# Two-layer mixer model on one core: reordering the second block's gates, roots, convolutions and parked loads round its quarter products

## The reference

```python
def hybrid_mixer(h, lower_bound, w_in, conv_w, ...):
    proj = h @ w_in                       # 1024 x 8192
    xa, ga, q, f, v, g, m_a, m_b = jnp.split(proj, SPLIT_POINTS, axis=-1)
    xa = causal_depthwise_conv(xa, conv_w, conv_b)        # 4 taps
    y_a = rg_lru(xa, w_r, b_r, w_i, b_i, lam) * jax.nn.gelu(ga)
    ...
    sig = jax.nn.sigmoid(zf)
    log_f = jnp.log(jnp.maximum(lb + (1.0 - lb) * sig, F_MIN))
    kf = (1.0 - lb) * jax.nn.sigmoid(-zf)
    o = rms_norm(hgrn2_chunkwise(qf, kf, log_f, vf), hg_norm)
    y_b = o * jax.nn.silu(g)
    y = jax.nn.sigmoid(m_a) * y_a + jax.nn.sigmoid(m_b) * y_b
    return y @ w_out
# rg_lru: r, i = sigmoid(block products of x); log_a = -8 r softplus(-lam); a = exp(log_a)
#         u = sqrt(max(-expm1(2 log_a), 0)) * (i * x); h = scan(a, u)
```

## Time and profile before

| | us |
|---|---|
| median of 3 runs | 3155.71 (3154.32 to 3157.86) |
| the profiled execution's own time | 3158.05 |
| its span, first to last instruction | 3156.2 |
| PE busy | 2902.3 (92%) |
| DVE busy | 1993.8 (63%) |
| ACT busy | 1290.2 (41%) |
| POOL busy | 1279.4 (41%) |

### The profile page before, as it was taken

The page is one execution under the profiler, slowest core; times in us unless marked ns, Lnnn a source line. Parts: engine busy times, 40 slices in busy tenths (PEclk is TensorE's granted clock), DMA queues, the critical chain, the costliest instruction groups (busy, mean ns, idle before and its releaser), DMA issues.

```text
span 3156.2 us, 49864 instructions
## 1 busy us (share of the span) xinstructions
PE 2902.3 (92%) x20118; PEld 1811.5 (57%) x20118; DVE 1993.8 (63%) x3135; ACT 1290.2 (41%) x2321; POOL 1279.4 (41%) x1071
## 2 busy tenths in 40 slices
PE   7979998999879989998889989989987999999998
PEld 7529875874449658754555655654653444444444
DVE  2476897763589987645875666576564474444445
ACT  2353655653366646633444444443532222222222
POOL 2402472010604570002745646656553335555552
PEclk9999999999999999999999999999998999999999
DMA  7323241002202330021101101101113101111111
GB/s 247 135 66 108 97 144 55 15 18 107 97 1 81 128 104 16 25 87 60 54 27 41 67 27 54 54 27 54 55 41 147 54 17 58 49 51 53 54 54 74
DMA packets 50901, 213.49 MB, mean 68 GB/s; under 512 B 4681, under 2 KB 9969, under 8 KB 34033
## 3 DMA queue, kind: packets, MB, share of 16 engines
q1 hardware_dynamic: 42288, 195.63, 17.5%
q10 hardware_dynamic: 8384, 14.68, 1.4%
HBM read 190.36 MB, written 19.94 MB: 67 GB/s over the span
## 4 chain that ended last, share of the span: by engine, by line
PE 72%; DVE 19%; issue 4%; ACT 4%; DMA 1%; POOL 0%; ACTq 0%; SPq 0%; DVEq 0%; POOLq 0%
PE big L282 15%; PE big L283 14%; PE big L284 14%; PE banks L282 5%; PE banks L284 5%; PE banks L283 5%; PE banks L1175 3%; DVE arena L2002 2%; PE banks L1002 2%; DVE arena L2246 1%; PE big L674 1%; DVE arena L2385 1%; DVE arena L2336 1%; DVE arena L2226 1%; PE banks L677 1%
## 5 line engine op out<-in xcount | busy, mean ns | idle before, releaser
L644 POOL TENSOR_TENSOR w_lo<-stage,w_hi 128x512 bf16<-128x512 f32 x340 | 423.6, 1276 | 368.3 <-ACT w_hi L1373 368.1
L637 POOL CAST w_hi<-stage 128x512 bf16<-128x512 f32 x252 | 178.7, 749 | 793.7 <-PE big L284 600.4
L587 POOL TENSOR_TENSOR w_lo<-stage,w_hi 128x512 bf16<-128x512 f32 x180 | 256.6, 1436 | 351.2 <-ACT w_hi L1573 269.5
L282 PE MATMUL big<-w_hi,ht_hi 128*128 128x256 bf16 (+2 forms) x1280 | 353.3, 285 | 15.2 <-DVE arena L1833 4.7
L282 PE MATMUL big<-ht_hi,w_hi 128*128 128x512 bf16 x800 | 309.1, 386 | 49.4 <-ACT arena L1587 17.9
L283 PE MATMUL big<-w_lo,ht_hi 128*128 128x256 bf16 (+2 forms) x1280 | 353.0, 285 | 0.0
L284 PE MATMUL big<-w_hi,ht_lo 128*128 128x256 bf16 (+2 forms) x1280 | 352.9, 285 | 0.0
L283 PE MATMUL big<-ht_lo,w_hi 128*128 128x512 bf16 x800 | 308.8, 386 | 0.0
L284 PE MATMUL big<-ht_hi,w_lo 128*128 128x512 bf16 x800 | 308.3, 385 | 0.0
L282 PE MATMUL big<-arena,w_hi 128*128 128x512 bf16 (+1 forms) x728 | 232.1, 335 | 45.8 <-DVE arena L2355 21.9
L283 PE MATMUL big<-arena,w_hi 128*128 128x512 bf16 (+1 forms) x728 | 231.4, 334 | 0.0
(11 more groups left out here) (390 smaller groups left out, 7245.4 us busy)
## 6 DMA issues: line engine op xcount, KB each, us to landing
stage<-in_w SPq DMA_DIRECT2D x130, 1024.0 KB, 4.8
arena<-in_w_ada SPq DMA_DIRECT2D x48, 512.0 KB, 3.9
arena<-in_x SPq DMA_DIRECT2D x16, 512.0 KB, 7.4
xs<-arena SPq DMA_DIRECT2D x16, 512.0 KB, 2.6
arena<-xs SPq DMA_DIRECT2D x16, 512.0 KB, 8.5
gt<-arena ACTq DMA_DIRECT2D x16, 256.0 KB, 2.8
arena<-gt ACTq DMA_DIRECT2D x16, 256.0 KB, 2.6
out_x<-arena SPq DMA_DIRECT2D x8, 512.0 KB, 2.6
```

Source lines behind the costliest of these rows:

```text
L282: pe.matmul(out, ah, bh, start=start, stop=False, skip_group_check=onto)
L587: return pool.tensor_tensor(lo, x, hi, ALU.subtract)
L637: pool.tensor_copy(w_flat[0][:, w0 + c0:w0 + c1], stage[:, n % RAW_RING, c0:c1]).then_inc(s_w_hi_split, mark(s_w_hi_split, n, q))
L644: ins = pool.tensor_tensor(w_flat[1][:, w0 + c0:w0 + c1], stage[:, n % RAW_RING, c0:c1], w_flat[0][:, w0 + c0:w0 + c1], ALU.subtract)
```

## The change

Seven edits, all in the second block:

1. The reciprocal on DVE goes. ACT makes the reciprocal root as exp(-0.5 ln(x)): `mean_log` in step ss for c = 0 (in `ga`) and `root_power` in `mb` behind "u1"; for c = 1 both in the next `xa` behind "u1" (`reciprocal_root`). `normed_state` of c = 0 moves from behind c11 to behind c12 of `mb`.
2. The input gate's arithmetic on DVE is taken apart and put between levels 4, 5 and 6. ACT does tanh and exponential of a half right behind its gate. The tanh of the first half is kept in `KT_`.
3. The two roots in `ga` are parted: the first behind "u2", the second behind "p5". The gelu of `ga` moves into `mb` behind "u1".
4. In `xa`, `y2_low(b-1, 0)` moves from behind c11 to behind c22 on DVE, and `y2_high(b-1, 0)` from "u1" to "u2" on ACT.
5. In `f`, the second convolution is cut in two halves, behind c11 and behind c22. ACT's second `forget` moves behind "u1" of `q`.
6. For `b` = 0: ACT copies the first half of `xa` out before it makes further sums; DVE makes the low parts of sum t1 before the first convolution, runs `forget` inside `q` (behind c22 and c12) and the second convolution behind `q`. The high and low parts of the second half of the convolution move into `v`.
7. Of the parked tiles four are loaded at the end of the last `mb`, two in the last `ma` behind "p5", with a semaphore of their own, and the tiles' places are swapped accordingly.

```diff
-        Y2_AT = [27648, 28672, 12288, 29704, 16384, 18432, 6144, 7168]
+        Y2_AT = [27648, 28672, 16384, 18432, 12288, 29704, 6144, 7168]
...
             def first_two(part, g):
-                pe.wait_ge(s_y2_in, when(s_y2_in))
                 for p, ks in ((0, range(4)), (1, range(2))):
+                    if p:
+                        pe.wait_ge(s_y2_rest, when(s_y2_rest))
+                    else:
+                        pe.wait_ge(s_y2_in, when(s_y2_in))
...
+            def functions(c, b, func, start=512):
+                act.wait_ge(s_c_out, when(s_c_out, c, b, "c12"))
+                act.wait_ge(s_p_out, when(s_p_out, c, b, "c21"))
+                for m, x0 in enumerate((0, start)):
+                    y = {"q": QE, "ga": YS, "mb": IT, "gg": FG, "ma": TH}[c][m][:, x0:T]
+                    act.activation(y, y, func).then_inc(...)
+            def tanh_r(b, m):
+                act.activation((KT_, TH[1])[m], R_[m], ACT.Tanh, scale=...)
...
+            def mean_log(b, c):
+                for half in range(2):
+                    act.activation(KT_[half], tile("t", "hs", b, c, "ss", half), ACT.Ln, scale=1.0 / P, bias=s_(S_EPS))
+            def reciprocal_root(b, c):
+                mean_log(b, c)
+                root_power(b, c)
+            def root_power(b, c):
+                act.activation(KT_, KT_, ACT.Exp, scale=-0.5)
@@ scalar, b == 0 @@
-                    sums_to_tt(0, "t2", "t3", "t4")
+                    sums_to_tt(0, "t2")
+                    evac(XAP[:, 0, 3:1027], ACT.Copy, "xa", 0, 0)
+                    sums_to_tt(0, "t3", "t4")
+                    evac(XAP[:, 1, 3:1027], ACT.Copy, "xa", 0, 1)
+                    parts_high(SEVEN[0], (0, 1, 2))
+                    parts_high(SEVEN[0], (3, 5))
+                    sums_to_tt(1, "t2")
+                    parts_high(SEVEN[0], (4,))
+                    parts_high(SEVEN[0], (6,))
                     for c in range(2):
+                        if c:
+                            sums_to_tt(1, "t3", "t4")
+                            act.wait_ge(s_gemm, when(s_gemm, "f", 0, 1))
+                            for g in range(2):
+                                sums_to_tt(g, "t1")
...
@@ scalar, b > 0 @@
-                    seven("xa", b, ACT.Copy, u1=lambda: y2_high(b - 1, 0), c21=lambda: y2_high(b - 1, 1))
+                    seven("xa", b, ACT.Copy, u1=lambda: reciprocal_root(b - 1, 1), u2=lambda: y2_high(b - 1, 0), c21=lambda: y2_high(b - 1, 1))
...
-                    for c in range(2):
-                        forget(b, c)
+                    forget(b, 0)
...
-                seven("q", b, ACT.Silu)
+                seven("q", b, ACT.Silu, u1=(lambda: forget(b, 1)) if b else None)
@@ scalar, gates @@
+                    if n == 0:
+                        tanh_r(b, 0)
                     evac(IT[n], ACT.Sigmoid, "i", b, n, bias=v_("b_i", 2 * b + n))
+                    if n == 1:
+                        tanh_r(b, 1)
+                    act.activation(R_[n], R_[n], ACT.Exp, scale=...)
-                seven("ga", b, ACT.Gelu_apprx_tanh, hgrn, u2=roots)
+                seven("ga", b, ACT.Copy, hgrn, u2=lambda: root(0), p5=lambda: root(1))
+                def between():
+                    root_power(b, 0)
+                    functions("ga", b, ACT.Gelu_apprx_tanh, 0)
-                seven("mb", b, ACT.Sigmoid, hgrn)
+                seven("mb", b, ACT.Sigmoid, hgrn, u1=between, u2=lambda: act.wait_ge(s_rg_dve, when(s_rg_dve, "ha", b, 1)), c21=y2_load if b == 3 else None)
-                seven("ma", b, ACT.Sigmoid, hgrn, c21=y2_load if b == 3 else None)
+                seven("ma", b, ACT.Sigmoid, hgrn, p5=y2_load_rest if b == 3 else None)
+            reciprocal_root(3, 1)
@@ vector @@
             def normed_state(b, m):
-                step(dve.reciprocal(KT_, KT_))
                 dve.scalar_tensor_tensor(OO, OO, v_("hg_norm", 0), KT_, ALU.mult, ALU.mult)
@@ vector, b == 0 @@
-                    conv_2(0, 0)
                     dve.wait_ge(s_gemm, when(s_gemm, "f", 0, 1))
                     for g in range(2):
                         sum_low(g, "t1", TSB[g])
-                    for c in range(2):
-                        forget(0, c)
+                    conv_2(0, 0)
+                    seven("q", 0, c22=(lambda: forget(0, 0),), c12=(lambda: forget(0, 1),))
                     conv_2(0, 1)
-                    seven("q", 0)
@@ vector, b > 0 @@
-                    seven("xa", b, c11=(lambda: y2_low(b - 1, 0), lambda: gated_state(b - 1, 1)), c22=(lambda: recurrent(b - 1, 1),), c12=...)
+                    seven("xa", b, c11=(lambda: gated_state(b - 1, 1),), c22=(lambda: y2_low(b - 1, 0), lambda: recurrent(b - 1, 1)), c12=...)
-                    seven("f", b, c11=(lambda: conv_2(b, 1),))
+                    seven("f", b, c11=(lambda: conv_2(b, 1, range(2)),), c22=(lambda: conv_2(b, 1, range(2, TAPS_2)),))
@@ vector, gates @@
-                seven("v", b, hgrn)
-                for u in range(4):
-                    hgrn(*hsteps[4 + u])
+                seven("v", b, hgrn, c11=(lambda: xs_low(1),))
+                hgrn(*hsteps[4])
+                hgrn(*hsteps[5])
+                input_gate(0)
+                hgrn(*hsteps[6])
+                one_less_square(0)
+                hgrn(*hsteps[7])
+                input_gate(1)
+                one_less_square(1)
-                seven("mb", b, hgrn, c11=(lambda: normed_state(b, 0),))
+                seven("mb", b, hgrn, c12=(lambda: normed_state(b, 0),))
```

More of the change, by code:

```diff
@@ L1692, in hgrn @@
                             freed(s_hgrn_act, "ho", *key, half)
-                    elif st == "ss":
-                        for half in range(2):
-                            act.wait_ge(s_hgrn, when(s_hgrn, *key, half))
-                            act.activation(KT_[:, half * 512:(half + 1) * 512], tile("t", "hs", *key, half)[:, :], ACT.Sqrt, scale=1.0 / P, bias=s_(S_EPS)).then_inc(s_hgrn_act, mark(s_hgrn_act, "o_rms", b, c, half))
-                            freed(s_hgrn_act, "hs", *key, half)
-                seven("v", b, ACT.Copy, hgrn)
+                    elif st == "ss" and c == 0:
+                        mean_log(b, 0)
+                seven("v", b, ACT.Copy, hgrn, u1=lambda: xs_high(1))
+                act.wait_ge(s_rg_dve, when(s_rg_dve, "xc", b, 1))
+                act.wait_ge(s_dve_setup, when(s_dve_setup, "sp8"))
                 for n in range(2):
-                    act.wait_ge(s_rg_dve, when(s_rg_dve, "xc", b, 1))
                     evac(R_[n], ACT.Sigmoid, "r", b, n, bias=v_("b_r", 2 * b + n))
+                    if n == 0:
+                        if b:
+                            act.wait_ge(s_hgrn_dve, when(s_hgrn_dve, "y2_a", b - 1, 1))
+                        else:
+                            act.wait_ge(s_t_lo, when(s_t_lo, "b2", 0, "t1"))
+                        tanh_r(b, 0)
                     if b:
@@ L2419, in _, with xs_low @@
                     normed_state(b - 1, 1)
-                    seven("xa", b, c11=(lambda: y2_low(b - 1, 0), lambda: gated_state(b - 1, 1)), c22=(lambda: recurrent(b - 1, 1),), c12=(lambda: y2_low(b - 1, 1),))
+                    seven("xa", b, c11=(lambda: gated_state(b - 1, 1),), c22=(lambda: y2_low(b - 1, 0), lambda: recurrent(b - 1, 1)), c12=(lambda: y2_low(b - 1, 1),))
                     conv_2(b, 0)
-                    seven("f", b, c11=(lambda: conv_2(b, 1),))
+                    seven("f", b, c11=(lambda: conv_2(b, 1, range(2)),), c22=(lambda: conv_2(b, 1, range(2, TAPS_2)),))
                     seven("q", b, c11=(lambda: forget(b, 0), lambda: forget(b, 1)))
-                for c in range(2):
+                def xs_low(c):
                     dve.wait_ge(s_rg_act, when(s_rg_act, "xs_hi", b, c))
                     dve.tensor_tensor(XS[1][:, c, :], XC[c], XS[0][:, c, :], ALU.subtract).then_inc(s_rg_dve, mark(s_rg_dve, "xs_lo", b, c))
+                xs_low(0)
                 def blocks(x, h):
```

88 lines of the change are left out of this document (45 added, 43 removed).

## The result

The changed kernel takes 3098.69 us (median of 4 runs, 3097.95 to 3101.14); the kernel before took 3155.71 in the same session (median of three runs; a fourth, at 4996.81, is left out as a slow one). The ratio is 0.982 with a 95% interval of 0.9801 to 0.9839, so 1.8% faster. The forecast was 3090, with 3068 to 3112 around it. The profiled execution took 3101.14 us, its span is 3099.3.

What follows compares the result with a forecast made beforehand. PE, busy 92% of the span, was taken as the bound: its work plus its gaps. Terms 25.6 + 30.4 + 3.9 - 5.5 + 12 = 66.4 us off 3158.05 gave 3091.7, by the median 3089.4, predicted 3090 (own range 3080 to 3102; with rivals 3068 to 3112).

Steps and rivals of the forecast that it cites:

- `ga`: 25.6 forecast: PE's four waits for the "p5" copy in `ga` go whole: 17.9 us plus 7.7 of lower clock.
- `mb`: 30.4 forecast: In `mb`, PE's waits for DVE's level 0 go with the reciprocal: 17.4 us plus 13.0 of lower clock.
- gaps in `mb` or `ga` that are only shorter: Sign named in advance as showing the prediction wrong: gaps in `mb` or `ga` shortened instead of gone.
- The slack of 1.3 us: In `mb`, DVE's level 0 would be ready at 1645.1, PE arriving at 1646.4.
- `xa`, `f`, `q`: 3.9 forecast: Last three parts: DVE's chain waits for ACT, POOL's weights bound next; gain 3.9 us, ends 0 and 19.
- the one wait of 3 to 4 us for POOL ahead of `q`: Parts two to four: the gaps of 3.9 + 2.4 us come back as this wait, with the same clock loss.
- The start: -5.5 forecast: First part: a new wait of about 6 us at level 0 for DVE's `qf`; loss 5.5 us, ends -8 and +2.
- The tail: 12 forecast: Behind the last `ma`: parked tiles end no wait, first token tile comes earlier; gain 12 us, ends 9 and 16.
- is split at 2407.2: Tail: POOL, started with the end of `ma`, finishes `o3` then, leaving PE 1.8 us idle.
- its third rival: POOL falls behind, slowed beside DVE by 8.7 us per chunk in `xa`, `f`, `q`: 3168 us, chance 0.04.
- the one for the tail: Sign: the tiles end no wait; `o3` and `y2_low(3, 1)` do, with under 6 us together.
- The rival in which ACT is the bound: ACT's added logarithms, exponentials and table loads delay copies PE waits for, 3 us x 7: 3111 us, chance 0.2.

Runs made afterwards that it cites:

- Experiments 3 to 5: Kernel after with edit 3 undone (3099.14 us), with DVE's half of edit 2 undone (3114.04 us), and with both undone (3113.0 us).
- Experiment 6: Kernel after with the state root of c = 0 by Sqrt and DVE's reciprocal again in all four parts: 3129.33 us.
- Experiments 7 and 12: Kernel after with looser waits ahead of `f` (3089.86 us); with those, a convolution of b=0 earlier, ACT making `o3`'s high parts, convolutions halved over `f` (3078.69 us).
- experiment 9: Kernel after with the state root of the last step (3,1) alone by Sqrt and DVE's reciprocal again: 3096.71 us.
- experiment 10: Kernel after with all six parked tiles loaded at the end of `ma` again, the two semaphores of edit 7 kept: 3099.57 us.
- experiment 5: Kernel after with edit 3 and DVE's half of edit 2 both undone: 3113.0 us.

## Why the prediction was right, and where it was not

The median of 3098.69 lies 9 us above the forecast of 3090 and inside the forecast's own 3080 to 3102.

**`ga`: 25.6 forecast, 25.9 measured.** Counted between step tr and step ss of c = 0, the four gains are 6.1, 6.0, 7.5 and 6.2 us. The mechanism was put down to edits 2 and 3 together. Experiments 3 to 5 part them: edit 3 adds nothing once edit 2 is there, DVE's half of edit 2 carries 10.0 us even with edit 3 in place, and 12.3 us stay when both are undone. The order on ACT in the first `ga` of the kernel after:

```profile
1616.43 1.06 ACT L1756 ACTIVATE arena<-arena 128x1024 f32<-128x1024 f32 x1
1617.39 0.58 ACT L1591 ACTIVATE arena<-big 128x512 f32<-128x512 f32 x1
1618.39 1.05 ACT L1756 ACTIVATE arena<-arena 128x1024 f32<-128x1024 f32 x1
```

The whole part starts 7 us later than before. Less these 7 us, DVE was done with its products at 1605.6 (1612.6), where 1604 to 1608 was forecast, and the copy of p5, which stands between the roots, came at 1610.4 (1617.4), where 1610 to 1611 was forecast.

**`mb`: 30.4 forecast, 27.9 measured.** Of the gap of 4.3 us 0.5 is left in each of the four parts, 2.0 us together, since DVE ended level 0 at 1647.7 and not before PE. By the letter of the prediction ("gaps in `mb` or `ga` that are only shorter") this is a miss, though the lower clock behind it is gone. The slack of 1.3 us that the prediction counted was 1.8 too large: level 0 took 5.0 us on DVE (1642.8 to 1647.7) and not 4.1, two of its operations running at 1.6 us, and began 0.9 us later than counted. Experiment 6 shows the same sum from the other side, 27.7.

**`xa`, `f`, `q`: 3.9 forecast, 5.8 measured.** Counted from step tr of c = 1 to step tr of the next part, the three gave 2.3, 0.9 and 2.6. In the first `xa` DVE's multiply stood 31.8 us behind that step and stands 31.3 behind it now, 0.5 us earlier where 0.7 was taken. The forecast's argument held so far: ACT ended the chain, with the second table load, and the weights of `q` were the next bound. ACT in the first `xa` of the kernel after:

```profile
1711.78 1.28 ACT L1658 ACT_TABLE_LOAD   x1
1713.07 1.27 ACT L1658 ACTIVATE arena<-banks,small 128x512 f32<-128x512 f32 x2
1714.35 1.28 ACT L1667 ACT_TABLE_LOAD   x1
1715.65 1.06 ACT L1667 ACTIVATE arena<-arena 128x1024 f32<-128x1024 f32 x1
```

The logarithm and the exponential each bring a load of 1.28 us. The Trainium skill, "ScalarE: Activation LUTs", section "Table sets: the hidden batching unit", has one load for the two; this trace has two, and the measurement decides. By the page's rule the root would have been ready 1.3 us earlier.

But the one wait of 3 to 4 us for POOL ahead of `q` came as two: 3.1 for ACT's first copy of `f`, which still waits for `y2_low(b-1, 1)`, and 0.9 to 2.1 for POOL. Experiments 7 and 12 show three bounds that stand within 4 us of one another in these parts: ACT's copy, DVE's convolutions, POOL's low parts.

**The start: -5.5 forecast, -7.1 measured.** The place and the size of the wait were right (6 us, it was 6.2, ended by `qf`), and `qf` ended at 1568.2, within the forecast's 1567 to 1569. So was the reason why the early copy of `xa` gives almost nothing: the forget gate frees PE at 1530.1, where 1530.4 was forecast. The forecast had a range of 3 to 7 us for where level 1 would come and took 5.5; the clock of 0.54 over 10 us behind the wait put it at the far end.

**The tail: 12 forecast, 5.7 measured.** This is the term that was mis-sized. PE came to the wait for `o3` 14.8 us behind step ss, as forecast (2405.4 is 14.9), and stood 9.8 us where 1.8 was forecast. The step that failed is that `o3` "is split at 2407.2", as in the kernel before, "POOL having started with the end of `ma`". POOL started at that moment, but took 24.3 us and not 16.4 (experiment 9). The forecast took the reciprocal out of DVE's 6.5 us, during which POOL had run free, put products in its place, and slowed only DVE by it ("up to 2.2 us" each), not POOL. The last low part, which it had ended 22.7 us behind step ss (2413.2), ended at 23.5. Both answer to these rows of DVE in the kernel after, the last low part and the first addition:

```profile
2359.44 2.08 DVE L2447 TENSOR_TENSOR arena<-arena 128x1024 bf16<-128x1024 f32 x1 [1.12 <-ACT arena L1633]
2370.62 1.22 DVE L2573 TENSOR_TENSOR arena<-arena,big 128x1024 f32<-128x1024 f32 x1 [9.09 <-PE big L285]
```

The Trainium skill, "SBUF — State Buffer", section "Who interferes with whom", has a DVE instruction with two SBUF inputs contend with a POOL instruction that reads SBUF, and calls contention on the ports that they share an exclusive lock. The trace agrees: POOL's low parts take 2.1 us each (8.42 for 4) where they took 1.1 (4.48 for 4) beside DVE's reciprocal. The prediction named this mechanism in its third rival, and weighed it there for `xa`, `f` and `q` only.

What edit 7 gave was also not what the forecast thought. Of the 5.7 us, 5.1 are there with the loads issued late (experiment 10), when PE starts behind four of the six tiles, and 0.6, no more than the spread, come with the early issue. The 5.1 are the second semaphore's: in the kernel before the fourth tile landed at 2403.8 and the sixth at 2408.6, and PE waited for all six, 16.4 us; in experiment 10 it waits 11.5, until the fourth.

**The sum.** 25.9 + 27.9 + 5.8 - 7.1 + 5.7 = 58.2, less the 1.4 behind the first addition, gives 56.8; the spans differ by 56.9, and 66.4 was forecast. The tail is 6.3 of the 9.5 us between them. It was partly luck that the rest is so small: 2.5 too much in `mb` and 1.6 at the start stand against 1.9 too little in `xa`, `f` and `q`. Of the signs that the prediction named, the one for the tail failed too: `o3` and `y2_low(3, 1)` were to end waits of under 6 us together, and `o3` alone ended 9.8. The rival in which ACT is the bound did not come: its second table load did, but no copy of `mb` was late by it.

## What to carry to other kernels

When a long one-operand instruction leaves DVE's order, ask not only who waits for DVE but who ran beside it: here POOL's sixteen operations took 7.9 us longer, and the tail gave 5.7 us where 12 were expected. A transfer that is issued earlier is worth what the next bound leaves of it (0.6 us or 7.6 for the same edit), so relieve that bound first. And when gaps of four parts repeat, cut the trace at the same instructions in both kernels: it gives each edit a term of its own, free of most of what the rest of the program does from run to run (up to 1.7 us of it stays in a stretch here).

## What the runs showed of the hardware

- DVE and POOL slow each other in both directions. DVE's products of 128x1024 took 1.22 to 1.23 us alone, 2.06 to 2.18 beside POOL's low parts and 1.5 to 1.6 beside its casts. POOL's low parts of 128x512 took 1.1 us alone and 2.1 beside DVE's products, its casts 0.57 (2.28 for 4) and 1.56 (6.25 for 4).
- The same wait is followed by the lower clock in one run and not in another. Behind the wait of 1.0 us at a level of the third part the clock stayed full in the kernel after and fell in experiment 6 (two stretches of 6 us, columns as in the first section):

```profile
1999.90:2005.90 6.00, 5.92 (x90) 5.92 (x91) 4.59 (x6) 0.00 (x0) 4.76 (x4) 1.00 0.50 165
```

```profile
2011.80:2017.80 6.00, 6.00 (x62) 6.00 (x63) 4.55 (x6) 0.00 (x0) 4.65 (x4) 0.72 0.52 172
```

  Of experiment 5's four waits of 2.4 us two were followed by it (0.72 over 6 us behind the second, 1.00 behind the first). The price here, 0.28 x 6.0 = 1.7 us, is the spread that some stretches show.
- A logarithm behind which an exponential follows brings two table loads of 1.28 us, with 0.01 to 0.02 us between load and instruction.
